# Norm sums of five half chunks from token-major x, forget logits beside V, five down pieces begun early

## The reference

```
h = RMSNorm(x);  p = h @ W_in -> q, k, v (8 heads x 64), f (8 logits), u, sv (512 each), gates (2 x 1024)
c = cumsum(log_sigmoid(f + b_f));  A = softmax(q.k/8 + c_t - c_s, causal) v
B = gelu(u) * (W_s layernorm(gelu(sv)) + b_s)          # windows of 128 tokens
x = x + (sigmoid(g_a) * (A @ w_a) + sigmoid(g_b) * (B @ w_b)) @ w_o
x = x + relu(RMSNorm(x) @ w_up)^2 @ w_down             # 4096 wide
out = RMSNorm(x)
```

## Time and profile before

| | |
|---|---|
| median of 3 runs | 1166.07 us (1164.69 to 1166.37) |
| profiled execution | 1166.1 us, its span (slowest core, first to last instruction) 1164.5 us |
| PE / PEld (weight loads) busy | 1123.4 / 569.7 us |
| DVE / ACT / POOL busy | 503.1 / 507.5 / 246.3 us |
| DMA | 85.43 MB |

### The profile page before, as it was taken

One profiled execution on the slowest core, in us unless ns is written; L12 is line 12 of the kernel. 1 busy time (PEld: TensorE's weight loads), 2 busy tenths in 40 slices (PEclk: granted clock), 3 DMA queues, 4 the chain that ended last, 5 costly groups with the idle time before them and its releaser, 6 DMA issues.

```text
span 1164.5 us, 22275 instructions; the slowest of 8 cores (1158.0 to 1164.5 us)
## 1 busy us (share of the span) xinstructions
PE 1123.4 (96%) x7598; PEld 569.7 (49%) x7735; DVE 503.1 (43%) x881; ACT 507.5 (44%) x702; POOL 246.3 (21%) x271
## 2 busy tenths in 40 slices
PE   7989999999999999999999999999999999999995
PEld 3445565565555555444444444444444444444444
DVE  3556634523211123775222475334444333334655
ACT  2344768888798886343222342111111111113332
POOL 4000100000000002436222004333333333333330
PEclk9999999999999999999999999999999999999998
DMA  8943631211325412206120834040403122130123
GB/s 176 260 133 111 181 94 58 70 43 50 78 64 99 83 24 35 48 2 135 32 52 1 188 111 73 1 73 1 73 7 66 28 46 43 31 68 21 69 86 122
DMA packets 35262, 85.43 MB, mean 73 GB/s; under 512 B 5568, under 2 KB 15904, under 8 KB 31744
## 3 DMA queue, kind: packets, MB, share of 16 engines
q0 software_dynamic: 10208, 45.86, 20.4%
q1 hardware_dynamic: 24656, 38.10, 11.3%
q10 hardware_dynamic: 288, 0.03, 0.0%
HBM read 99.88 MB, written 13.17 MB: 97 GB/s over the span
## 4 chain that ended last, share of the span: by engine, by line
PE 88%; DMA 4%; DVE 4%; issue 2%; ACT 1%; POOL 0%; SPq 0%; DVEq 0%; ACTq 0%; POOLq 0%
PE pss L365 88%; DMA WK<-wproj 2%; DMA QpT<-scrq 1%; DVE ostg L383 1%; DMA QpT<-QT 1%; DMA xbuf<-xown 1%; DVE x1T L377 0%; DVE hown L383 0%; ACT PT L369 0%; DVE yst L377 0%; DVE VP L387 0%; DVE slo L377 0%; POOL WV L393 0%; DVE kst L387 0%; SPq L393 0%
## 5 line engine op out<-in xcount | busy, mean ns | idle before, releaser
L369 ACT ACTIVATE PT<-pss 128x1024 bf16<-128x1024 f32 (+1 forms) x288 | 272.5, 975 | 84.9 <-PE pss L365 78.8
L377 DVE TENSOR_TENSOR x1T<-pss,x1T 128x512 f32<-128x512 f32 (+1 forms) x232 | 155.7, 673 | 232.5 <-PE pss L365 212.1
L365 PE MATMUL pss<-aT,fdn 128*128 128x512 bf16 (+1 forms) x1070 | 228.7, 368 | 1.9 <-POOL aT L377 1.0
L365 PE MATMUL pss<-h2T,fup 128*128 128x512 bf16 x1003 | 225.0, 379 | 1.1
L369 ACT ACTIVATE rl<-pss 128x512 f32<-128x512 f32 x128 | 76.4, 597 | 304.1 <-PE pss L365 304.1
L377 POOL TENSOR_TENSOR aT<-rl 128x512 bf16<-128x512 f32 x128 | 137.2, 1073 | 262.7 <-ACT rl L369 259.0
L365 PE MATMUL pss<-QpT,KpT 86*128 86x512 bf16 (+3 forms) x640 | 167.3, 348 | 5.9 <-DVE hown L383 2.6
L365 PEld LDWEIGHTS pss<-aT,fdn 128*128 128x128 bf16 x1088 | 107.1, 99 | 116.8 <-issue 1.2
L365 PEld LDWEIGHTS pss<-h2T,fup 128*128 128x128 bf16 x1024 | 100.2, 98 | 120.5
L365 PEld LDWEIGHTS pss<-VP,PT 128*128 128x128 bf16 x2176 | 99.9, 97 | 56.8 <-issue 9.5
L365 PE MATMUL pss<-VP,PT 128*128 128x65 bf16 x2176 | 113.1, 193 | 3.7 <-DVE yst L377 3.6
(11 more groups left out here) (139 smaller groups left out, 1058.3 us busy)
## 6 DMA issues: line engine op xcount, KB each, us to landing
xbuf<-xprev POOLq DMA_DIRECT2D x16, 512.0 KB, 11.2
xres<-xown SPq DMA_DIRECT2D x32, 256.0 KB, 3.8
fup<-w_up POOLq DMA_DIRECT2D x8, 1024.0 KB, 9.6
fdn<-w_down POOLq DMA_DIRECT2D x8, 1024.0 KB, 10.8
xbuf<-xown POOLq DMA_DIRECT2D x12, 512.0 KB, 7.0
out<-ostg SPq DMA_DIRECT2D x24, 256.0 KB, 2.1
scrt<-kst SPq DMA_DIRECT2D x32, 128.0 KB, 2.4
KpT<-scrt SPq DMA_DIRECT2D x8, 512.0 KB, 4.7
```

What stands on the lines that cost most here:

```text
L365: S.op("pe", lambda e, a=(out, lhsT, rhs, start, stop): e.matmul(a[0], a[1], a[2], start=a[3], stop=a[4]), r, w)
L369: S.op("act", lambda e, a=(out, in_, func, scale): e.activation(out=a[0], in_=a[1], func=a[2], scale=a[3]), r, w)
L377: S.op(eng, lambda e, a=(out, in0, in1, op): e.tensor_tensor(a[0], a[1], a[2], a[3]), r, w)
```

## The change

For positions 3 to 7 a second copy of x, tokens on partitions, is loaded in blocks of 128 tokens x 1024 (`xtm`, two buffers of 512 KB in the place of `sq`). ScalarE squares a block in one ACTIVATE and gives the row sum (`ssq`); on the four sums per partition Ln and Exp work on 128x4; VectorE builds two diagonal matrices, rstd in bf16 and its rest (`dgh`, `dgl`), and TensorE spreads them with two passes against ones in place of eight; ScalarE copies the result to rstd. Blocks 0 and 1 of a half chunk are fetched ahead, the fetch of block 2 is issued on GpSimd's queue once block 0 is squared, that of block 3 once block 1 is.

The forget columns are put into WV (520 columns), and a V unit becomes two of 264 and 256 columns; `f_q` is gone. The order in `chunk_list` is new: V units come first, then K and Q. In the prologue x is loaded before the small tensors, on two queues; the first head's four loads are issued together, and the second head's on ScalarE's queue. One Q unit moves from the prologue into the fill. At the end five pieces are begun ahead in place of three, the ones passes lag by four pieces in place of two in the first half, and six banks are used in place of three.

```diff
...
+        xload(0, "sp")
...
+        def tmload(pos, blk):
+            own, I = order[pos]
+            ld("pool", xtm[blk % 2][:], xtm_d[own, I * 4 + blk], B("xtm%d" % (blk % 2)))
         def sq_q(pos):
             i_ = pos % 2
+            if pos >= TM0:
+                def mt(blk):
+                    def q():
+                        xt, xB = xtm[blk % 2], B("xtm%d" % (blk % 2))
+                        S.op("act", lambda e, a=(xt[:], xt[:], ssq[:, blk:blk + 1]): e.activation(out=a[0], in_=a[1], func=AF.Square, accum_out=a[2]), [xB], [xB, B("ssq")])
+                        if blk < 2:
+                            tmload(pos, blk + 2)
+                        elif blk == 3 and pos < 7:
+                            tmload(pos + 1, 1)
+                    return (0.0, q)
+                return [mt(blk) for blk in range(4)]
...
+        TM0 = 3
+        def rms_tm(pos):
+            i_ = pos % 2
+            def small():
+                act(rtm[:], ssq[:], AF.Ln, [B("ssq"), B("epsT")], [B("rtm")], scale=1.0 / 1024.0, bias=epsT[:, 0:1])
+                act(rtm[:], rtm[:], AF.Exp, [B("rtm")], [B("rtm")], scale=-0.5)
+                cp("dve", rhi[:], rtm[:], [B("rtm")], [B("rhi")])
+                tt("dve", rlo[:], rtm[:], rhi[:], ALU.subtract, [B("rtm"), B("rhi")], [B("rlo")])
+                i4 = identb[:, :].unsqueeze(1).broadcast_to([128, 4, 128])
+                for dg, rr, rn in ((dgh, rtm, "rtm"), (dgl, rlo, "rlo")):
+                    tt("dve", dg[:, :].rearrange("p (b t) -> p b t", t=128), i4, rr[:, :].unsqueeze(2).broadcast_to([128, 4, 128]), ALU.mult,
+                       [B("identb"), B(rn)], [B("xtm0")])
+            def q():
+                pb = fbank()
+                mm(ps(pb), onesb[:], dgh[:], True, False, [B("onesb"), B("xtm0")], [PB[pb]])
+                mm(ps(pb), onesb[:], dgl[:], False, True, [B("onesb"), B("xtm0")], [PB[pb]])
+                acopy(rstd[i_][:], ps(pb), [PB[pb]], [B("rstd%d" % i_)])
+                rdone.add(pos)
+                if pos < 7:
+                    tmload(pos + 1, 0)
+            return [(0.0, small)], [(2 * PASS, q)]
...
+        def v_mm(pos, blk, half, pv, kc):
+            w0, w = (0, 264) if half == 0 else (264, 256)
+            mm(pss[:, pv * 512:pv * 512 + w], hsl(pos, kc, blk * 128, 128), WV[:, kc * 520 + w0:kc * 520 + w0 + w], kc == 0, kc == 7,
+               [hbuf(pos, kc), B("WV%d" % (kc // 2))], [PB[pv]])
+        def v_evict(pos, blk, half, pv):
             own, I = order[pos]
             gb = (4 * own + I) * 4 + blk
...
-            own, I = order[pos]
             ci = 4 * own + I
-            def q():
-                pb = fbank()
-                for blk in range(4):
-                    for kc in range(8):
-                        mm(pss[:, pb * 512 + blk * 8:pb * 512 + blk * 8 + 8], hsl(pos, kc, blk * 128, 128), wf[:, kc * 8:(kc + 1) * 8],
-                           kc == 0, kc == 7, [hbuf(pos, kc), B("wf")], [PB[pb]])
...
+            if half == 0:
+                tt("dve", zt[:, blk * 8:(blk + 1) * 8], pss[:, pv * 512 + 256:pv * 512 + 264], bfb[:, blk * 8:(blk + 1) * 8], ALU.add, [PB[pv], B("bfb")], [B("zt")])
+                if blk == 3:
+                    def fin():
+                        act(et[:], zt[:], AF.Exp, [B("zt")], [B("et")], scale=-1.0)
+                        act(spt_all[:, ci * 32:(ci + 1) * 32], et[:], AF.Ln, [B("et")], [B("spt%d" % ci)], bias=1.0)
+                        fdone.add(pos)
+                    later(2, fin)
+            cp("dve", VP4[:, gb, :, 65 * half:65 * half + 64], pss[:, pv * 512:pv * 512 + 256].rearrange("p (q d) -> p q d", d=64), [PB[pv]], [B("VP%d" % gb)])
+        def v_q(pos, blk):
+            return (unit_q(lambda pv, kc: v_mm(pos, blk, 0, pv, kc), lambda pv: v_evict(pos, blk, 0, pv), 1, 0.92) +
+                    unit_q(lambda pv, kc: v_mm(pos, blk, 1, pv, kc), lambda pv: v_evict(pos, blk, 1, pv), 1, 0.88))
...
+            vb = [[fbank(), fbank()] for _ in range(4)]
             for kc in range(8):
                 for blk in range(4):
-                    mm(ps(vb[blk]), hsl(pos, kc, blk * 128, 128), WV[:, kc * 512:(kc + 1) * 512], kc == 0, kc == 7,
-                       [hbuf(pos, kc), B("WV%d" % (kc // 2))], [PB[vb[blk]]])
-            run(f_q(pos))
+                    for half in range(2):
+                        v_mm(pos, blk, half, vb[blk][half], kc)
+            for half in range(2):
+                for blk in range(4):
+                    v_evict(pos, blk, half, vb[blk][half])
             flush_late()
...
-        headload(0, 1)
         run(weave(kq_q(1, 1, False) + kq_q(1, 2, False), sq_q(2), 2))
         run(fin_tr(0, 0) + fin_tr(0, 1) + fin_tr(0, 2))
-        headload(0, 2)
-        headload(1)
+        headload(0)
+        headload(1, "act")
         ring[:] = [5, 6, 7, 4]
         run(rms_q(2))
-        run(weave(kq_q(1, 3, False) + kq_q(0, 1, True) + kq_q(0, 2, True) + kq_q(0, 3, True), stt_q(2), 1))
+        tmload(3, 0)
+        tmload(3, 1)
+        run(weave(kq_q(1, 3, False) + kq_q(0, 1, True) + kq_q(0, 2, True), stt_q(2), 1))
...
             if c == 1:
-                qs += weave(kq_q(o, 0, False) + kq_q(o, 0, True), sq_q(e), 2)
+                qs += weave(kq_q(0, 3, True) + [("pair", (0, 3))] + v_q(o, 0) + v_q(o, 1), sq_q(e), SQ1)
                 qs += ev(lambda: xload(o + 2))
-                qs += f_q(o) + rms_q(e)
-                qs += weave(v_q(o, 0) + v_q(o, 1) + v_q(o, 2) + kq_q(o, 1, False), stt_q(e), 1)
-                vs = [v_q(o, 3)]
+                ra, rb = rms_tm(e)
+                qs += ra + v_q(o, 2) + rb + v_q(o, 3)[:1]
+                qs += weave(v_q(o, 3)[1:] + kq_q(o, 0, False) + kq_q(o, 0, True), stt_q(e), 2)
             else:
-                qs += weave(kq_q(o - 2, 3, True) + [("pair", (c - 1, 3))] + kq_q(o, 0, False) + kq_q(o, 0, True) + v_q(o, 0), stt_q(e), 1)
-                qs += f_q(o)
-                vs = [v_q(o, 1), v_q(o, 2), v_q(o, 3)]
+                qs += kq_q(o - 2, 3, True) + AFTER.pop(0) + [("pair", (c - 1, 3))]
+                qs += weave(v_q(o, 0) + v_q(o, 1) + v_q(o, 2) + v_q(o, 3), stt_q(e), 1)
...
+            if c == 1:
+                qs += kq_q(e, 0, False) + fin_tot(c) + kq_q(o, 1, False) + fin_cum(c)
+            else:
+                qs += kq_q(o, 0, False) + fin_tot(c) + kq_q(o, 0, True) + fin_cum(c) + kq_q(e, 0, False)
+            k1, q1 = kq_q(e, 1, False), kq_q(o, 1, True)
+            if c > 1:
+                qs += fin_tr(c, 0) + fin_tr(c, 1) + fin_tr(c, 2)
+                t1 = kq_q(o, 1, False) + [("ready", c)] + k1 + q1 + [("pair", (c, 1))]
+            else:
+                t1 = k1 + fin_tr(c, 0) + q1[:1] + fin_tr(c, 1) + q1[1:] + fin_tr(c, 2) + [("ready", c), ("pair", (c, 1))]
             if c < 3:
-                qs += weave(t1, sq_q(o + 2), 2)
-                qs += rms_q(o + 2)
+                qs += weave(t1, sq_q(o + 2), 1)
+                ra, rb = rms_tm(o + 2)
+                q2 = kq_q(o, 2, False)
+                qs += ra + q2 + rb
+                rest = kq_q(e, 2, False) + kq_q(o, 2, True) + [("pair", (c, 2))] + kq_q(o, 3, False) + kq_q(e, 3, False)
+                st, sm_ = stt_q(o + 2), sq_q(e + 2)
                 mix = []
...
+                for z in range(8):
+                    mix += [st[z]] + ([sm_[z - 4]] if z >= 4 else [])
+                qs += weave(rest[:5], mix[:4], 1) + weave(rest[5:], mix[4:], 2)
                 if c < 2:
                     qs += ev(lambda: xload(o + 4))
-                qs += kq_q(e, 3, False)
-                qs += rms_q(e + 2)
+                ra, rb = rms_tm(e + 2)
+                qs += ra
+                AFTER.append(rb)
...
             def finish():
-                ones_pass(6)
-                ones_pass(7)
+                for kc in range(8 - lag, 8):
+                    ones_pass(kc)
...
-            ahead = 3 if I == 3 and c0 == 0 else 0
+            bk = [4, 5, 6, 0, 1, 2] if I == 3 else [4, 5, 6]
+            ahead = 5 if I == 3 and c0 == 0 else 0
+            lag = 4 if ahead else 2
...
-                pb = 4 + dc % 3
+                pb = bk[dc % len(bk)]
                 down_mm(pb, dc, ns, c0, w, 4 if dc < ahead else 0, 8)
-                if dc >= 2:
-                    ones_pass(dc - 2)
+                if dc >= lag:
+                    ones_pass(dc - lag)
...
```

More of the change, by code:

```diff
@@ L167, in build @@
     xown_d = dt_in("xown", [4, 128, 8 * 512])
-    wproj_d = dt_in("wproj", [5, 128, 8 * 512])
-    wf_d = dt_in("wf", [128, 64])
+    xtm_d = dt_in("xtm", [2, 16, 128, 1024])
+    wproj_d = dt_in("wproj", [4, 128, 8 * 512])
+    wvf_d = dt_in("wvf", [128, 8 * 520])
     wmrg_d = dt_in("wmrg", [8, 128, 24 * 128])
@@ L245, in build @@
         rsv = [palloc("rsv%d" % i, 1, F32) for i in range(4)]
+        ssq, rtm, rlo = [palloc(n, 4, F32) for n in ("ssq", "rtm", "rlo")]
+        rhi = palloc("rhi", 4, BF16)
         rec = [palloc("rec%d" % i, 4, F32) for i in range(2)]
@@ L299, in build @@
```

(64 more changed lines are left out.)

59 lines of the change are left out of this document (24 added, 35 removed).

## The result

The changed kernel took 1196.32 us (median of 4 runs, 1194.07 to 1198.63) against 1165.38 for the one before in the same comparison: ratio 1.025, 95% interval 1.0226 to 1.0273. By the ratio it is slower by 29 us (by the two medians 31) where 4 us faster was predicted, far outside the range of 1152 to 1168. The profiled execution took 1194.1 us, its span 1192.5, which is 28.0 more than before.

What follows compares the result with a forecast made beforehand. TensorE was taken to bound the kernel (1123.4 of 1164.5 us busy). Terms -6.5 - 3.8 - 0.5 + 0.6 - 3.4 = -13.6 us, with + 8.0 + 1.7 for new waits and clock, gave -3.9: 1162.2 us, range 1152 to 1168.

Steps and rivals of the forecast that it cites:

- Passes taken off: Norm sums at positions 3 to 7: two ones passes each in place of eight, 6.5 us off TensorE.
- Logits beside V: Forget logits put into V's passes: 0.64 us less per half chunk, counted for six in the fill, 3.8 us.
- Start and opening: Start gains 0.5 us from earlier x; opening of attention loses 0.6, bounds 2 either way, scores starting near 68 us.
- The wait that was added: TensorE waits for exponentials queued behind late blocks' squares on ScalarE, positions 4 to 7: 8.0 us in sum.
- so I take 4.2: Landing time of an xtm block after its issue, around positions 6 and 7: 4.2 us.
- the prediction's own rule: Each us more of landing time adds about 1 us of wait at each of positions 4 to 7.
- Clock: Lowered TensorE clock after waits, counted once for positions 4 to 7: 1.7 us, bounds 0 and 3 times.
- The work on ScalarE hardly changes: ScalarE needs four squares of 1024 per half chunk, about 1.02 us each, so its work stays nearly the same.
- Rstd itself ... is covered by two K or V units: Rstd's two small ACTIVATEs and four small VectorE instructions, 2.5 us, hide behind two units on TensorE.
- rival 3: Blocks share queue and engines and land after 7.0 us: waits 19.2 us, low clock, 1176.8 us; chance 0.14.
- Tail: Last down projection: passes fill gaps and the clock is kept, 3.4 us gained, bounds 1.7 and 3.4.

Runs made afterwards that it cites:

- r3: z2 with the squares spread, Ln and Exp half a unit later and norm passes moved; no transfers for positions 5 to 7, old tail: 1159.38 us, ratio 0.9928.
- y3: Kernel before with the logits beside V alone, old order, prologue, norm sums and tail; some logits wrong: ratio 0.9979.
- x3: Changed kernel with the old norm sums at all positions; new order, logits, prologue and tail kept: 1168.32 us, ratio 1.001.
- z3: y3 with its logits mended, plus the new tail: 1165.24 us, ratio 0.9957.
- y1: Changed kernel with the second head's four loads back on SP's queue: ratio 1.0231.
- x2: Changed kernel with xtm in bf16 in four buffers, every block fetched half a chunk ahead: 1184.72 us, ratio 1.0152.
- y2: Changed kernel with the three transposes of the logit rows set apart by half K units: ratio 1.0239.
- x1: Changed kernel without transfers of blocks 2 and 3; squares reread blocks 0 and 1, rstd wrong at positions 3 to 7: 1178.44 us, ratio 1.0097.
- z2: y4 with its logits mended, without the transfers of positions 5 to 7 (rstd wrong there): 1168.71 us, ratio 1.0001.
- r1: x1 with a third staging buffer for the logit rows from the attention loop on: 1172.28 us, ratio 1.0038.
- r4: r3's spread order with all transfers and the new tail: 1168.46 us, ratio 1.0008.
- y4: y3 plus the new norm sums at positions 4 to 7, prefetched in bf16; some logits wrong: ratio 1.0095.
- x4: Kernel before with the new tail alone: 1165.25 us, ratio 0.9981.
- q1: Changed kernel, whole, with a third staging buffer for the logit rows from the attention loop on: ratio 1.0253.
- r2: z3 plus the new norm sums at positions 6 and 7 alone, prefetched in bf16, squares spread: 1158.56 us, ratio 0.9925.

## Why the prediction was wrong, point by point
- **Passes taken off.** Right in size. The 64 V passes of the prologue start 111 ns apart (18.59 to 25.57 us; 110 predicted). r3 has 5.2 us fewer norm passes than y3 and the same tail, and takes 0.9928 in place of 0.9979 of before, 5.9 us less, with an interval of some 3 us either way: it agrees with the term once nothing else waits. That cover failed is the error, not the term.
- **Logits beside V.** Predicted 3.8 us, measured 2.4 alone (y3; interval 0.6 to 4.3). The new order of units gave no more; x3 is 6 us behind z3 by order and prologue; the profiles point to the order inside the loop, and which part of it is open.
- **Start and opening.** 0.6 us lost by the forecast. The first scores were expected near 68 us and started at 69.90: the last small load of the first head was issued at 66.92 (67.06 before), not 2.5 us sooner, and TensorE waited 4.89 us for 2.58. Exponential 0 came 1.2 us sooner, exponential 1 3.7 later and exponential 3 2.2 later (82.2 for 80.0 us), a little beyond the bound of 2. Not by ScalarE's loads: moving the second head's back changed nothing (y1). x2, with four blocks loaded ahead of the first head, waits 8.6 us here.
- **The wait that was added: the step that failed first.** The prediction counted 8.0 us at positions 4 to 7: 0.4, 2.5, 3.1 and 2.0. TensorE waited 3.0, 6.9 and 5.7 us for PT at positions 4, 5 and 7, 1.2 at position 3, which the prediction had in the opening with 0.5, and at position 6 4.5 us for the staging copy (y2, without that, has 6.2 for PT there). x1 measures 18 us for the late blocks, clock and half of the traffic included. "so I take 4.2" was too low by 0.5 us only, in the mean of the eight blocks in question. The issue, too, came 0.7 us later than counted, since the reading of the row sum and the issue itself stand behind the square. Together 6.4 us from square to landing in place of 5.2, which by the prediction's own rule, 1 us for each us at four positions, gives 12.8 us; the rest, most of it at position 5, is a count of the steps that was too kind, and no run takes it apart. The mechanism (ScalarE's order, block 2 ahead of the exponentials) was right at positions 4, 5 and 7. The 3.2 us of the Trainium skill ("DMA: Bandwidth & Descriptors", Anatomy of one DMA) are below the smallest landing here, 3.5; the measurement decides.
- **Clock: mis-sized most.** Counted once, 1.7 us, bounds 0 and 3 times. It fell with each of six waits, and at positions 3 to 7 it cost some 12 us, more than the 8.0 us of waits that were forecast. In z2 waits of 1.9 and 1.1 us were followed by 5 us at 0.50.
- **"The work on ScalarE hardly changes", and "Rstd itself ... is covered by two K or V units": failed.** The sum of the work is nearly the same, its place is not. Four squares at one a step hold ScalarE for 2.2 us a step where TensorE needs 1.5, and Ln and Exp stand right behind them. Spread, the same work cost nothing that is seen: z2 to r3 gained 8.5 us with the same transfers, passes and tail, and the wait of 1.90 us is gone; the edit moves the norm passes and some units as well, so the spreading alone wasn't measured. VectorE's four small instructions are covered only if VectorE is free, and it stood at the staging copy: 7 us (x1 to r1). Nothing in the prediction looked at the three transposes in a row.
- **The transfers' price to others: left out but for rival 3's landing.** 10.5 MB through the same engines slow the head loads and those of x. (The page of before has a row that the prediction passed over, 16 loads of 512 KB of `xbuf<-xprev` with a median landing of 11.2 us.) In the changed kernel TensorE waits 3.5 us for a head's load at 107 us, in r4 8.16 us. y4 against z2, 11 us, and r4 against r3, 9 us and the tail, both leave no other difference but transfers (and the mended logits of z2).
- **Tail.** Right: in the first half a single wait of 0.70 us at the first ones pass (0.9 predicted), full clock, 3.6 us gained between w_o and the end (3.4 predicted); x4's interval by itself, 0.8 to 3.7 us, agrees.

Rival 3 was nearest, and right in the sign only: it needed landings of 7.0 us, and the blocks in question had 4.7; what it left out made the rest. The trace adds up as follows. At positions 3 to 7 TensorE waited 16.8 us for PT, 4.5 for the staging copy and 3.5 for a head's load (waits of over 0.8 us; before the change none), and lost some 12 by the clock; the opening lost 3.6 by wait and clock. With the 13.7 us of the passes and the tail taken off as forecast that makes 26.7 of the 28.0 us. The runs can't be added in this way, since one wait hides another (y2, q1).

## What to carry to other kernels
A saving of passes is worth its length only if what replaces them keeps its place: spread what is new over an in-order engine at a rate that leaves it time for each step, and look at what stands behind it there. Price a transfer also by what it does to the landings of others, above all where small loads that TensorE needs share the engines. The norm sums at two positions, with eight blocks, came out 4 us under z3 (r2), at four positions, with sixteen, 6 us over it (r4). r2 fetches its first four blocks while the engines are 0.98 busy; they land after 8 to 12 us, but are needed only much later, and no head load is waited for. Count what the granted clock takes after each wait: here it was as dear as half of the waits. A wait taken away while a longer one stands behind it shows no gain; test each cause with the others removed.
